# Taking the gates of a pair apart: one step at a time between the next pair's weights

## The reference

```python
def conv_gated_ffn(x, w_up, w_gate, conv_w, conv_b, w_down):
    u = x @ w_up                                     # (512, 2816)
    g = causal_dwconv(x @ w_gate, conv_w, conv_b)    # 3 taps, per feature
    return (jax.nn.silu(g) * u) @ w_down
```

## Time and profile before

| | us |
|---|---|
| median of 3 runs | 1791.28 (1789.99 to 1794.4) |
| profiled execution | 1790.65 |
| its span, first to last instruction | 1788.9 |
| TensorE busy | 1742.5 (97%) |
| VectorE busy | 1150.7 (64%) |
| ScalarE busy | 896.7 (50%) |
| mean granted TensorE clock | 0.987 of full speed |

### The profile page before, as it was taken

One profiled execution on the slowest core, in us unless ns is written; L12 is line 12 of the kernel. 1 busy time (PEld: TensorE's weight loads), 2 busy tenths in 40 slices (PEclk: granted clock), 3 DMA queues, 4 the chain that ended last, 5 costly groups with the idle time before them and its releaser, 6 DMA issues.

```text
span 1788.9 us, 24379 instructions
## 1 busy us (share of the span) xinstructions
PE 1742.5 (97%) x9933; PEld 1449.4 (81%) x9933; DVE 1150.7 (64%) x1812; ACT 896.7 (50%) x1408; POOL 40.2 (2%) x53
## 2 busy tenths in 40 slices
PE   9999998999999999999999888999999999999999
PEld 7877998888888887777788887888898876778766
DVE  6778886644433565887786666643368867657674
ACT  6889755433332355666564444432246454533542
POOL 0000100000000000000200000000000000000000
PEclk9999999999999999999999988999999999999999
DMA  5374265755446643311234353223322222132211
GB/s 212 129 219 112 82 198 155 246 166 165 130 151 190 189 130 118 95 48 60 71 115 145 118 162 128 99 95 107 103 85 92 94 60 71 63 102 85 69 60 47
DMA packets 59663, 213.22 MB, mean 119 GB/s; under 512 B 7072, under 2 KB 7328, under 8 KB 56608
## 3 DMA queue, kind: packets, MB, share of 16 engines
q1 hardware_dynamic: 56096, 169.73, 28.5%
q0 software_dynamic: 3456, 41.95, 8.9%
HBM read 207.45 MB, written 44.04 MB: 141 GB/s over the span
## 4 chain that ended last, share of the span: by engine, by line
PE 79%; DVE 11%; ACT 7%; issue 2%; DMA 1%; SPq 0%; ACTq 0%; DVEq 0%
PE bank L618 79%; DVE wl L2161 3%; ACT tmp L1437 2%; DVE tmp L2152 2%; ACT wh L1437 2%; DVE tmp L2149 1%; DMA wraw<-in_wstream 1%; DVE HL L2161 1%; DVE sqr L2152 1%; ACT taps L1437 1%; DVE XL L2161 1%; PE bank L1382 0%; DMA wraw<-tw 0%; ACT HH L1437 0%; DVE sbl L2161 0%
## 5 line engine op out<-in xcount | busy, mean ns | idle before, releaser
L2161 DVE TENSOR_TENSOR wl<-wraw,wh 128x1024 fp32r<-128x1024 f32 (+1 forms) x294 | 355.3, 1219 | 274.2 <-ACT wh L1437 273.5
L618 PE MATMUL bank<-XH,wh 128*128 128x512 f32 (+1 forms) x1424 | 526.9, 370 | 3.0 <-DVE wl L2161 1.0
L618 PE MATMUL bank<-XL,wh 128*128 128x512 f32 (+1 forms) x1424 | 517.0, 363 | 0.0
L618 PE MATMUL bank<-XH,wl 128*128 128x512 f32 (+1 forms) x1424 | 516.9, 363 | 0.0
L1437 ACT ACTIVATE wh<-wraw 128x1024 fp32r<-128x1024 f32 (+1 forms) x294 | 306.5, 1052 | 318.4 <-PE bank L618 265.8
L618 PEld LDWEIGHTS bank<-XH,wh 128*128 128x128 f32 x1424 | 268.7, 189 | 55.9 <-issue 9.4
L618 PEld LDWEIGHTS bank<-XH,wl 128*128 128x128 f32 x1424 | 268.7, 189 | 42.8
L618 PEld LDWEIGHTS bank<-XL,wh 128*128 128x128 f32 x1424 | 269.0, 189 | 39.8 <-issue 0.7
L618 PE MATMUL bank<-HL,wh 128*128 128x256 f32 (+1 forms) x740 | 223.4, 345 | 34.9 <-DVE sqr L2152 34.9
L618 PE MATMUL bank<-HH,wh 128*128 128x256 f32 (+1 forms) x740 | 223.2, 344 | 0.0
L618 PE MATMUL bank<-HH,wl 128*128 128x512 f32 (+1 forms) x580 | 202.9, 350 | 0.0
(11 more groups left out here) (375 smaller groups left out, 2438.3 us busy)
## 6 DMA issues: line engine op xcount, KB each, us to landing
wraw<-in_wstream SPq DMA_DIRECT2D x256, 512.0 KB, 3.6
wraw<-tw SPq DMA_DIRECT2D x80, 256.0 KB, 3.2
tw<-in_w POOLq DMA_DIRECT2D x6, 1536.0 KB, 12.6
tw<-in_w POOLq DMA_DIRECT2D x4, 2048.0 KB, 15.5
wraw<-in_wstream SPq DMA_DIRECT2D x22, 256.0 KB, 2.9
tw<-in_w POOLq DMA_DIRECT2D x4, 1024.0 KB, 10.6
tw<-in_w POOLq DMA_DIRECT2D x6, 512.0 KB, 7.9
tw<-tw POOLq DMA_DIRECT2D x2, 1536.0 KB, 7.3
```

The costliest lines, as they stand in the source:

```text
L618: return pe.e.matmul(o, l, r, start=start, stop=stop, skip_group_check=True)
L2161: return dve.e.tensor_tensor(o, x, h.bitcast(F32), ALU.subtract)
```

## The change

Three things change; no computation does.

1. The run of `gated` is cut into `bias`, `silu`, `high` (ScalarE) and `taps`, `product`, `low` (VectorE), and each is placed by itself between the feeds and recombinations of the next pair. `first_combined(0, p)` now stands ahead of the taps, and `three_combined(0, p)` ahead of the second tile's product and of both low parts.
2. A third buffer `third` joins the two of `sqr`; the two outputs of up of pair p are numbers 2p and 2p + 1 of these three, counted round. The first evacuation of a pair therefore waits for a product of two pairs back, the second for the product of tile f - 2.
3. The first pair gets four empty places in the stream where the later pairs have the rest of gate f - 1, so that it too is 56 places or seven units. The pairs of layer 0 now all start on a unit's first block. Everything from there to layer 1's first pair moves by half a unit; in layer 1 the first pair starts in the middle of a unit, and pairs 1 to 6 do so before and after. From there on all units begin with the same blocks as before, one unit further on.

`combined` (the counts of the sums) lists the same sequence, cut at another place. TensorE's program is unchanged.

```diff
@@ ffn_order
-        if p:
-            out += [(gate, k, f - 1) for k in range(4, KD)]
+        out += [(gate, k, f - 1) for k in range(4, KD)] if p else [None] * 4
@@ place
+            m.third.append(sb(ph, f"third{layer}", [128, S]))
+    m.ub = [[[(m.sqr + [t])[(2 * p + j) % 3] for j in range(2)] for p in range(FT // 2)] for t in m.third]
@@ scalar_program, ffn (pair loop)
+            if p:
+                second_out(1, tg, p - 1)
             feed_group(up, range(KD), [f])
             if p:
-                pair_gated(p - 1, 0)
+                pair_bias(p - 1, 0)
             first_out(0, up, p)
             if p:
                 feed_group(gate, range(4, KD), [f - 1])
-                pair_gated(p - 1, 1)
-            feed_group(tu, range(16), [p])
+            feed_group(tu, range(4), [p])
+            if p:
+                pair_bias(p - 1, 1)
+            feed_group(tu, range(4, 12), [p])
+            if p:
+                silu(f - 2)
+            feed_group(tu, range(12, 16), [p])
+            feed_group(gate, range(4), [f])
+            if p:
+                silu(f - 1)
             second_out(0, tu, p)
-            feed_group(gate, range(KD), [f])
+            feed_group(gate, range(4, KD), [f])
+            feed_group(up, range(4, KD), [f + 1])
+            if p:
+                high(f - 2)
             first_out(1, gate, p)
-            feed_group(up, range(4, KD), [f + 1])
-            feed_group(tg, range(16), [p])
-            second_out(1, tg, p)
+            feed_group(tg, range(8), [p])
+            if p:
+                high(f - 1)
+            feed_group(tg, range(8, 16), [p])
@@ vector_program, ffn (pair loop)
+            if p:
+                three_combined(1, p - 1)
             feed_group(up, range(KD), [f])
-            if p:
-                gated(f - 2, sqr[0], m.gb[0])
             first_combined(0, p)
             if p:
+                taps(f - 2, m.gb[0])
+                last_combined(1, p - 1)
+                dve.wait_ge(s.u_c, combined(layer, p - 1, 1, 5))
                 feed_group(gate, range(4, KD), [f - 1])
-                last_combined(1, p - 1)
-                gated(f - 1, sqr[1], m.gb[1])
-            feed_group(tu, range(16), [p])
+            feed_group(tu, range(12), [p])
+            if p:
+                product(f - 2, m.ub[layer][p - 1][0])
+                taps(f - 1, m.gb[1])
             three_combined(0, p)
-            feed_group(gate, range(KD), [f])
+            feed_group(tu, range(12, 16), [p])
+            feed_group(gate, range(4), [f])
+            if p:
+                product(f - 1, m.ub[layer][p - 1][1])
+            feed_group(gate, range(4, KD), [f])
+            feed_group(up, range(4, KD), [f + 1])
             first_combined(1, p)
-            feed_group(up, range(4, KD), [f + 1])
+            if p:
+                low(f - 2)
             last_combined(0, p)
             dve.wait_ge(s.u_c, combined(layer, p, 0, 5))
-            feed_group(tg, range(16), [p])
-            three_combined(1, p)
+            feed_group(tg, range(8), [p])
+            if p:
+                low(f - 1)
+            feed_group(tg, range(8, 16), [p])
```

More of the change, by code:

```diff
@@ L1556, in gated, with silu, high, pair_bias @@
+        def silu(f):
+            u = tmp[2 * f % 4]
+            act.wait_ge(s.f_conv, FT * layer + f + 1)
             fn(u[:, :], u[:, :], ACT.Silu).then_inc(s.f_silu, 1)
-            act.wait_ge(s.f_h, n + 1)
-            fn(HH[:, f, :], v[:, :], ACT.Copy).then_inc(s.f_hi, 1)
-        def pair_gated(p, odd):
+        def high(f):
+            act.wait_ge(s.f_h, FT * layer + f + 1)
+            fn(HH[:, f, :], tmp[(2 * f + 1) % 4][:, :], ACT.Copy).then_inc(s.f_hi, 1)
+        def pair_bias(p, odd):
@@ L1561, in pair_gated @@
             act.wait_ge(s.u_c, combined(layer, p, 1, 4 + odd))
-            gated(2 * p + odd, m.gb[odd])
+            bias(2 * p + odd, m.gb[odd])
         def first_out(g, mat, p):
+            if g == 0 and p >= 2:
+                act.wait_ge(s.f_h, FT * layer + 2 * p - 2)
             act.wait_ge(s.stream, w.done(mat, KD - 1, 2 * p))
-            fn((sqr, m.gb)[g][0][:, 0:256], bank[3 * g][:, 0:256], ACT.Copy).then_inc(s.u_e, 1)
+            fn((m.ub[layer][p], m.gb)[g][0][:, 0:256], bank[3 * g][:, 0:256], ACT.Copy).then_inc(s.u_e, 1)
@@ L1590, in ffn @@
             if f == 2 * PAIRS[layer]:
-                pair_gated(PAIRS[layer] - 1, 0)
+                pair_bias(last, 0)
                 feed_group(gate, range(4, KD), [f - 1])
-                pair_gated(PAIRS[layer] - 1, 1)
+                pair_bias(last, 1)
+                silu(f - 2)
+                silu(f - 1)
+                high(f - 2)
+                high(f - 1)
             feed_group(gate, range(KD), [f])
             act.wait_ge(s.stream, w.done(gate, KD - 1, f))
-            gated(f, bank[gate_bank(f)])
+            bias(f, bank[gate_bank(f)])
+            silu(f)
+            high(f)
         table(LNEXP)
@@ L2347, in gated, with product, low @@
             stt(u[:, 2:S], bg[:, 0:S - 2], P(f"fcw{layer}", 3 * f), u[:, 2:S], ALU.mult, ALU.add).then_inc(s.f_conv, 1)
[L2348 to L2351, removed]
+        def product(f, bu):
+            dve.wait_ge(s.f_silu, FT * layer + f + 1)
+            tt(tmp[(2 * f + 1) % 4][:, :], tmp[2 * f % 4][:, :], bu[:, :], ALU.mult).then_inc(s.f_h, 1)
+        def low(f):
+            dve.wait_ge(s.f_hi, FT * layer + f + 1)
+            less(HL[:, f, :], tmp[(2 * f + 1) % 4][:, :], HH[:, f, :]).then_inc(s.f_lo, 1)
         def first_combined(g, p):
-            b, (o, _) = bank[3 * g:3 * g + 3], (sqr, m.gb)[g]
+            b, (o, _) = bank[3 * g:3 * g + 3], (m.ub[layer][p], m.gb)[g]
             dve.wait_ge(s.u_e, 4 * (pairs_before(layer) + p) + 2 * g + 1)
@@ L2367, in last_combined @@
         def last_combined(g, p):
-            q = (sqr, m.gb)[g][1]
+            q = (m.ub[layer][p], m.gb)[g][1]
             dve.wait_ge(s.stream, w.done(("up", "gate")[g] + str(layer), KD - 1, 2 * p + 1))
@@ L2393, in ffn @@
             if f == 2 * PAIRS[layer]:
-                gated(f - 2, sqr[0], m.gb[0])
+                taps(f - 2, m.gb[0])
+                last_combined(1, last)
+                dve.wait_ge(s.u_c, combined(layer, last, 1, 5))
                 feed_group(gate, range(4, KD), [f - 1])
-                last_combined(1, PAIRS[layer] - 1)
-                gated(f - 1, sqr[1], m.gb[1])
+                taps(f - 1, m.gb[1])
+                product(f - 2, m.ub[layer][last][0])
+                product(f - 1, m.ub[layer][last][1])
+                low(f - 2)
+                low(f - 1)
             feed_group(gate, range(KD), [f])
-            gated(f, bank[(2 + 2 * f) % 6], bank[gate_bank(f)])
+            taps(f, bank[gate_bank(f)])
+            product(f, bank[(2 + 2 * f) % 6])
+            low(f)
         for c in range(KD + 1 - PARTS[i + 1]):
```

33 lines of the change are left out of this document (18 added, 15 removed).

## The result

| | runs | median us | range us |
|---|---|---|---|
| before | 4 | 1790.94 | 1789.99 to 1794.40 |
| after | 4 | 1764.81 | 1761.28 to 1766.01 |

The ratio is 0.9847, with a 95% interval of 0.9828 to 0.9867. I had forecast 1743, with a range of 1736 to 1760: the direction was right, and the time lies above the range.

A forecast was written before the change was run, and what follows sets the result against it. TensorE was taken as the bound, busy 1742.5 of 1788.9 us, with eight stalls worth 55.3 us including the slower clock. Less 6.9 left over, 48.4 won from 1790.65 gave 1742.3, median 1743; range 1736 to 1760.

The forecast's parts named there:

- The stalls of layer 1: Waits before `last_product(0, p)` shrink to 0.79 us late per pair, 1.46 in the pair with the table load.
- The chain that I named: In layer 1's pairs, weights at block 20, product, taps, silu, evacuation, sum hold the remaining stall of 0.8 us.
- The clock: Rival: repeated idles of about 0.8 us in layer 1 keep the clock down, 16 us more, 1759; chance 0.11.
- I take 0, with -1 and +5 as ends: Cost in us of shifting all units between layer 0's pairs and layer 1's first pair by half a unit.
- the edits with no cost: Third buffer, `first_combined` ahead of the taps, `low` and `high` behind the sums, and the half-unit shift: taken as 0.
- the eight stalls: TensorE waits of 4.35 to 4.37 us before `last_product(0, p)`, two in layer 0, six in layer 1; 55.3 us to win.
- The rival that I had on the slower side: The half-unit shift puts a 1.14 us `wl` ahead of sums in some 64 units between the layers: 1816; chance 0.04.
- Layer 0's second pair: Pair 1: 1.5 us left over, 0.52 for the table load and 1 for late DMA, ends 0 and 4.
- The sum: Left over 5 x 0.79 + 1.46 + 1.5 = 6.9 us; won 48.4; 1742.3 for the profiled execution, median 1743.

The follow-up runs named there:

- The swap: The realigned kernel with the evacuation `second_out(0, tu, p)` put ahead of `silu(f - 1)` on ScalarE; 1740.67 us, ratio 0.9717.
- one unit made earlier: The changed kernel with weight unit 121 (last k of wq and wk, first of wv) rounded and split at the normalisation's start; 1750.88 us, ratio 0.9776.
- realigned: The changed kernel with four empty places at the end of layer 0's tiles instead of in layer 1's first pair; 1746.82 us, ratio 0.9748.
- gates whole: The realigned kernel with each gate's steps behind one another again, third buffer, moved sums and stream kept; 1785.64 us, ratio 0.9963.

## Why the prediction was wrong

**The stalls of layer 1: right.** I had forecast periods of 20.95 us and a lateness of 0.79, with 1.46 in the second pair. Measured are 21.02 and 21.03 (1005.44 to 1026.47), so 0.87, and in the second pair 1.42 idle and a period of 21.84, so 1.68. The chain that I named is the one that ends last, as the rows ahead of the wait at 1005.44 in the kernel after show. VectorE:

```profile
1000.26 1.23 DVE L2194 TENSOR_TENSOR wl<-wraw,wh 128x1024 fp32r<-128x1024 f32 x1 [1.16 <-ACT wh L1439]
1001.40 0.69 DVE L2185 TENSOR_TENSOR tmp<-tmp,third 128x512 f32<-128x512 f32 x1
1002.01 1.53 DVE L2182 SCALAR_TENSOR_TENSOR tmp<-acc_q,prm,tmp 128x511 f32<-128x511 f32 x2
1004.51 0.42 DVE L2185 TENSOR_TENSOR sqr<-third,bank 128x256 f32<-128x256 f32 x1 [0.97 <-ACT third L1439]
1004.96 0.42 DVE L2185 TENSOR_TENSOR third<-bank,sqr 128x256 f32<-128x256 f32 x1
```

And ScalarE:

```profile
1003.57 0.63 ACT L1439 ACTIVATE tmp<-tmp 128x512 f32<-128x512 f32 x1 [0.46 <-DVE tmp L2182]
1004.11 0.37 ACT L1439 ACTIVATE third<-bank 128x256 f32<-128x256 f32 x1
```

The pair starts at 991.61 (1005.44 less 0.87 less 12.96). From there the `wl`, the product, the taps, the silu, the evacuation and the two sums stand at 8.65, 9.79, 10.40, 11.96, 12.50, 12.90 and 13.35, each within 0.1 us of what I had laid out. So this number is no luck. The swap takes the silu out of the chain, and the wait goes. Layer 1 gained 36.9 us, its 33.98 and the 2.94 by which the second pair's wait shrank (4.36 to 1.42); I had 37.7.

**The clock: right.** The windows of the kernel after, from the second pair's wait to the last one, all show 1.00, with 0.61 us idle once in 21; the first of the five:

```profile
984.42:1005.44 21.02, 20.41 (x168) 20.20 (x168) 17.21 (x26) 11.77 (x17) 0.00 (x0) 1.00 0.55 175
```

So the rule of the Trainium skill that I had as a rival ("TensorE: Matmul & The Clock Gate", A second HAM failure mode: psum-queue depth-cycling) does not bite at this size of idle.

**"I take 0, with -1 and +5 as ends": the step that failed.** It stands under the edits with no cost, for the half-unit shift between the layers. It cost 16.1 us by the profile: 12.6 at `wq` and `wk`, and in the attention the 0.53 of the table plus the 2.94 that the second pair's wait had shrunk, 3.5 (with the shift taken out, the same stage took 272.98 us instead of 276.53). By the medians it was 16.2 and 18.0 in the two kernels without it. My reason was that TensorE idled only 11.5 us outside the eight stalls, so the stretch had cover. That argument is about work that moves on an engine with room. The shift did another thing: it changed which blocks share a unit, and so which hand-placed call makes a block. The four blocks of k = 7 crossed such a border, and they came a whole normalisation later. The rival that I had on the slower side was in the right stretch with the wrong mechanism: many small delays of a `wl`, where it was one large one and, in the attention, three of 0.84, 0.99 and 1.71 us. The rows of before could not have shown this wait; the table of units beside the four calls would have, and I had both.

**Layer 0's second pair: right in kind, too small.** I had taken 1.5 us there, with 4 as the end, and nothing for the first pair. Left over in layer 0 are 2 x 6.10 - 5.22 = 7.0 us: 0.51 in the first pair, 3.70 in the second, and a clock that then fell, which I had not counted in my 1.5:

```profile
289.50:300.00 10.50, 10.45 (x67) 10.46 (x68) 7.66 (x11) 4.01 (x8) 0.00 (x0) 0.74 0.49 151
```

2.7 of these 10.5 us are lost (10.5 times 0.26). In the kernel with one unit made earlier, with the same program in layer 0, 8.6 us were left, the waits of 3.66 and 2.06 and a clock of 0.84 behind each; in the realigned one, on the same chip, 3.8: its wait of 3.18 left the clock at 1.00, and layer 0 took 406.16 us. So the term is 3.8 to 8.6 us in three executions, and my end of 4 is near the least of them. The mechanism, raw weights that land late beside the copies, is in the rows of ScalarE; why one execution has it in the first pair and the next in the second stays open. The third pair has no wait, as I had said. (By the prediction's own steps ScalarE wants the second unit at 2.88 + 0.26 = 3.14 and not at 3.35; nothing in the sum hangs on it.)

**The sum.** 1742.3 plus 12.6 (`wq`), 3.5 (attention), 5.5 (layer 0), 0.7 (layer 1) and 1.4 (ahead of layer 0, where executions differ by that much) is 1766.0, the time of the profiled execution. With the shift taken out, the kernel runs in 1746.8, against my 1743.

## What to carry to other kernels

When padding or an added piece shifts a packed stream, list for every call that names a piece of it which unit it reaches before and after, and where the first block behind that border is consumed; a block that crosses such a border waits for the next call, however much room the engines have. A low idle total in the stages that a shift passes is no cover, because it says nothing about an order written by hand. Before a small difference is read from one execution, look at a second kernel that has the same program there: here layer 0 changed by 4.8 us between two of them. And when a chain of handoffs between two in-order engines sets a wait, look for the link in it that nobody needs yet: here one swap of neighbours gave 6 us.

## What the runs showed of the hardware that I had not expected

- The fall of the clock depends on more than the length of the idle ahead of it. In layer 1, with 0.61 us once in 21 it never fell; with 2.39 us it fell in four of five periods, at a price of 1.35 to 1.51 us; with 3.83 us (gates whole) in all five periods between the six waits (0.88 to 0.94), 25.54 to 26.91 us each; with 4.36 in the kernel before in each. In layer 0, a 3.18 us idle (realigned) left it at 1.00; one of 2.06 (one unit made earlier) did not, as this window behind it shows:

```profile
290.08:301.00 10.92, 10.92 (x78) 10.92 (x79) 8.95 (x14) 5.02 (x8) 0.00 (x0) 0.84 0.62 175
```

- So a stall of 2.39 us costs 4.0 us where the clock falls (24.17 less the 20.16 of a pair without loss) and 2.6 where it doesn't (22.80), and one of 0.61 costs 0.9: a stall costs more than its idle time says.
- The table load takes 1.28 us and the silu starts 1.29 us behind its start (283.55, 284.84); the rounding ahead of it had ended at 283.53. The Trainium skill ("ScalarE: Activation LUTs", What ACT_TABLE_LOAD costs) counts a drain on top, about 2.7 us in all; in these rows no drain stands ahead of the load or behind it.
